# A third place in the down ring, and an up half between the down units, in a two-layer MoE decoder trunk

## The reference, cut to what matters

```python
x = layer_norm(DN_ALPHA * x + mix, ln1_g[layer], ln1_b[layer])
ff = moe_ffn(...)                       # below
x = layer_norm(DN_ALPHA * x + ff, ln2_g[layer], ln2_b[layer])

def body(y, blk):                       # in moe_ffn, for each block of tokens of one expert
    tok, wt, e = blk
    xb = x[tok]
    hb = jax.nn.silu(xb @ w_gate[e]) * (xb @ w_up[e])
    return y.at[tok].add((hb @ w_down[e]) * wt[:, None]), None
```

## Time and profile before

| | us |
|---|---|
| median of 3 runs (1247.1 to 1247.83) | 1247.29 |
| the profiled execution, its own time | 1247.77 |
| its span in the profile | 1245.9 |
| PE busy in the span | 1186.4 (95%) |
| DMA moved | 445.64 MB, mean 358 GB/s |
| the share of the w_up_ring loads in the chain that ended last | 12% |

### The profile page before, as it was taken

How to read it: one execution, slowest core, us unless ns; L and a number is a source line. 1 busy time by engine, 2 the same in 40 slices (tenths; PEclk the granted TensorE clock), 3 DMA queues, 4 the chain that set the end, 5 groups by cost and what they waited for, 6 DMA issues and landing times.

```text
span 1245.9 us, 18133 instructions
## 1 busy us (share of the span) xinstructions
PE 1186.4 (95%) x7212; PEld 544.5 (44%) x7212; DVE 396.7 (32%) x892; ACT 298.3 (24%) x652; POOL 40.5 (3%) x110
## 2 busy tenths in 40 slices
PE   8998999999999999999879999999999999999985
PEld 5776754434334343433236565343443434343421
DVE  3757374222212121212233656421221212122213
ACT  3345332211212111211121353121221211121112
POOL 1005000000000000100000000000000000010000
PEclk9999999999999999999989999999999999999998
DMA  9407159999999999999993656899999999999993
GB/s 369 172 1 302 47 220 426 403 392 427 429 429 429 429 429 428 428 428 428 426 388 128 270 203 260 352 400 396 428 429 428 429 428 429 428 428 429 429 428 156
DMA packets 44336, 445.64 MB, mean 358 GB/s; under 512 B 8064, under 2 KB 9216, under 8 KB 18176
## 3 DMA queue, kind: packets, MB, share of 16 engines
q1 hardware_dynamic: 43984, 444.71, 85.6%
q10 hardware_dynamic: 304, 0.26, 0.1%
HBM read 443.91 MB, written 1.05 MB: 357 GB/s over the span
## 4 chain that ended last, share of the span: by engine, by line
PE 80%; DMA 12%; DVE 4%; ACT 1%; issue 1%; DVEq 0%; SPq 0%
PE psum L427 31%; PE psum L508 15%; DMA w_up_ring<-in_moe_up 12%; PE psum L515 4%; PE psum L2480 4%; PE psum L441 4%; PE psum L2329 4%; PE psum L1350 3%; PE psum L659 2%; PE psum L490 1%; PE psum L1661 1%; PE psum L1833 1%; PE psum L693 1%; PE psum L2486 1%; PE psum L1397 1%
## 5 line engine op out<-in xcount | busy, mean ns | idle before, releaser
L427 PE MATMUL psum<-w_up_ring,moe_x_selected 128*64 128x512 f32 x2048 | 458.7, 596 | 17.0 <-DMA w_up_ring<-in_moe_up 11.5
L427 PEld LDWEIGHTS psum<-w_up_ring,moe_x_selected 128*64 128x64 f32 x2048 | 141.4, 137 | 298.3 <-issue 287.4
L508 PE MATMUL psum<-w_down_ring,moe_hT 128*32 128x512 f32 x1920 | 219.7, 595 | 4.3 <-DMA w_down_ring<-in_moe_down 3.4
L1181 DVE TENSOR_TENSOR moe_out_low<-psum,moe_out_high 128x512 fp32r<-128x512 f32 x128 | 88.3, 691 | 365.4 <-ACT moe_out_high L931 365.4
L931 ACT CAST moe_out_high<-psum 128x512 fp32r<-128x512 f32 x128 | 74.8, 586 | 275.3 <-PE psum L508 217.0
L1173 DVE SCALAR_TENSOR_TENSOR moe_h<-moe_silu,moe_slot_gate,psum 128x256 f32<-128x256 f32 x64 | 30.7, 480 | 290.3 <-ACT moe_silu L915 290.0
L508 PEld LDWEIGHTS psum<-w_down_ring,moe_hT 128*32 128x32 f32 x1920 | 55.7, 109 | 135.1 <-issue 125.2
L915 ACT ACTIVATE moe_silu<-psum 128x256 f32<-128x256 f32 x64 | 24.6, 384 | 226.1 <-PE psum L427 226.1
L919 ACT COPY moe_hT<-psum 128x256 f32<-128x256 f32 x64 | 23.8, 373 | 181.6 <-PE psum L490 181.6
L515 PE MATMUL psum<-moe_out_high,moe_matchT 128*128 128x512 f32 x128 | 57.6, 450 | 2.9 <-DVE moe_out_low L1181 1.9
L2329 PE MATMUL psum<-w_up_ring,mixed_transposed 128*128 128x512 f32 x128 | 56.6, 594 | 0.7 <-ACT mixed_transposed L2104 0.7
(11 more groups left out here) (538 smaller groups left out, 997.8 us busy)
## 6 DMA issues: line engine op xcount, KB each, us to landing
w_up_ring<-in_moe_up SPq DMA_DIRECT2D x128, 2048.0 KB, 18.1
w_down_ring<-in_moe_down SPq DMA_DIRECT2D x60, 2048.0 KB, 19.1
w_up_ring<-in_ev_columns SPq DMA_DIRECT2D x4, 2048.0 KB, 16.1
w_up_ring<-in_od_w_in SPq DMA_DIRECT2D x4, 2048.0 KB, 18.1
w_up_ring<-in_ev_out SPq DMA_DIRECT2D x2, 2048.0 KB, 8.3
moe_first_down<-in_moe_down SPq DMA_DIRECT2D x2, 2048.0 KB, 9.9
w_up_ring<-in_od_w_out SPq DMA_DIRECT2D x2, 2048.0 KB, 7.7
moe_shared_weights<-in_shared_up SPq DMA_DIRECT2D x1, 2048.0 KB, 7.6
```

What stands on the lines that cost most here:

```text
L427: last = nc.tensor.matmul(k.psum[e * SLOTS:(e + 1) * SLOTS, bank, :], xsel[:, kk, own:own + SLOTS], up_view(par, e, kk), start=kk == 0, st ...
L508: last = nc.tensor.matmul(k.psum[e * CAPACITY:(e + 1) * CAPACITY, unit_bank[n], :], hT[:, e // 2, own:own + CAPACITY], places[e][:, j, :], ...
L1181: nc.vector.tensor_tensor(low[:, own], k.psum[:, unit_bank[n], :], high[:, own], ALU.subtract).then_inc(s.low, 1)
```

## The change

The norm's and the tokens' tiles become one tile (`norm_and_tokens`), whose 32 KB in a partition are two half places before and one whole place now. From the second quad on, that place is the first place of every odd double (`third_down`), filled up to the seventh quad (doubles 3 to 13) and with a semaphore of its own (`x.dn_norm`). So the first down load of a double has two places, taken in turn, and is issued one double earlier. The norm's gain and bias are loaded once it is free for good, in the seventh quad, behind 30a. On PE, `down` is split into `first_two`, `third` and `last_two`, and an up half stands between units 1 and 2: 2b in the first double of a quad, the next quad's 0b in the second; ACT's silu and DVE's product of that pair move between their second and third unit. `next_up` goes behind the two combines after the gather, except in the first quad, where a part of the shared expert's product moves behind it. The last double is as before.

```diff
+    k.norm_tokens = sb("norm_and_tokens", [P, 2, NT, D])
+    k.ln, k.x = k.norm_tokens[:, 0], k.norm_tokens[:, 1]
...
+    third_ring_down = [[third_down[:, e] for e in range(4)], ring_down[1]]
...
-        refill_up(4, 4, 0)
+        for half in range(2):
+            refill_up(4, 4, half)
         refill_down(2, 1, 4)
-        refill_up(4, 4, 1)
-        refill_up(5, 5, 0)
-        refill_up(5, 5, 1)
+        for half in range(2):
+            refill_up(5, 5, half)
         refill_up(6, 6, 0)
         refill_down(2, 0, 6)
-        sp.wait_ge(s.down, 8)
-        for i, src in enumerate((d.ln2_g, d.ln2_b)):
-            sp.dma_start(k.ln[0:QUARTER, i, :], ...)
+        refill_up(6, 6, 1)
+        refill_down(3, 0, 8, third_down, x.dn_norm)
...
-        def refills(q, final=False):
-            refill_up(4 * q + 2, 2, 1)
+        def refills(q):
             for half in range(2):
                 refill_up(4 * q + 3, 3, half)
-            if not final:
-                refill_up(4 * q + 4, 0, 0)
-            for half in range(2):
-                refill_down(2 * q + 1, half, 8 * q + 2 + 2 * half)
...
+            refill_up(4 * q + 4, 0, 0)
+            refill_down(2 * q + 2, 0, 8 * q + 2)
             refill_up(4 * q + 4, 0, 1)
+            refill_down(2 * q + 1, 1, 8 * q + 4)
             for half in range(2):
                 refill_up(4 * q + 5, 1, half)
             refill_up(4 * q + 6, 2, 0)
-            for half in range(2):
-                refill_down(2 * q + 2, half, 8 * q + 6 + 2 * half)
-        refills(QUADS - 1, final=True)
+        with sp.Fori(1, QUADS - 2) as q:
+            refills(q)
+            refill_down(2 * q + 3, 0, 8 * q + 6, third_down, x.dn_norm)
+            refill_up(4 * q + 6, 2, 1)
+            refill_down(2 * q + 2, 1, 8 * q + 8)
+        q = QUADS - 2
+        refills(q)
+        sp.wait_ge(s.down, 8 * q + 6)
+        for i, src in enumerate((d.ln2_g, d.ln2_b)):
+            sp.dma_start(k.ln[0:QUARTER, i, :], ...)
+        refill_up(4 * q + 6, 2, 1)
+        refill_down(2 * q + 2, 1, 8 * q + 8)
...
+            first_two(q, 0, ring_down, landed)
+            up(q, 2, 1)
+            last_two(q, 0, ring_down, landed)
...
-                next_up(q)
             for n in (2, 3):
                 combine(q, 0, n)
...
+                next_up(q, 0)
                 pe.wait_ge(s.gates_read, q + 2)
...
+                first_two(q, 1, third_ring_down, landed)
+                next_up(q, 1)
+                last_two(q, 1, third_ring_down, landed)
```

More of the change, by code:

```diff
@@ L767, in first_quad @@
             pe.wait_ge(s.matchT, 1)
-            down(0, 0, [[first_down[:, e] for e in range(4)], ring_down[1]], [[(x.dn_first, 16)], [(x.dn1, 16)]], begin=True)
+            places, landed = [[first_down[:, e] for e in range(4)], ring_down[1]], [[(x.dn_first, 16)], [(x.dn1, 16)]]
+            first_two(0, 0, places, landed)
             up(0, 2, 1)
+            last_two(0, 0, places, landed, begin=True)
             pe.wait_ge(s.low, 3)
@@ L776, in first_quad @@
             turn(0, 3)
-            next_up(0)
-            pe.wait_ge(s.shared_h, 1)
-            combine(0, 0, 2, begin=True)
-            combine(0, 0, 3, begin=True)
-            pe.wait_ge(s.gates_read, 2)
-            down(0, 1, [ring_down[0], [place[:, e] for place in (norm_down, token_down) for e in range(2)]],
-                 [[(x.dn0, 16)], [(x.dn_norm, 16), (x.dn_tokens, 16)]])
+            next_up(0, 0)
+            shared_up(0, range(6, KD)).then_inc(s.shared_up, 1)
+            pe.wait_ge(s.gates_read, 2)
+            places, landed = [ring_down[0], third_ring_down[0]], [[(x.dn0, 16)], [(x.dn_norm, 16), (x.dn_tokens, 16)]]
+            first_two(0, 1, places, landed)
+            pe.wait_ge(s.shared_h, 1)
+            for n in (2, 3):
+                combine(0, 0, n, begin=True)
+            next_up(0, 1)
+            last_two(0, 1, places, landed)
         def quad(q, final=False):
-            landed = lambda double: [[(dn[half], 16 * (2 * q + double))] for half in range(2)]
-            up(q, 0, 1)
+            landed = [[(dn[0], 16 * (q + 1))], [(dn[1], 32 * q)]]
             pe.wait_ge(s.low, 8 * q - 1)
@@ L821, in quad @@
                 turn(q, 3)
+                landed = [[(dn[0], 16 * (q + 2))], [(dn[1], 16 * (2 * q + 1))]]
+                first_two(q, 1, ring_down, landed)
+                for n in range(2):
+                    combine(q, 1, n)
+                third(ring_down, landed)
+                pe_unit(ring_down[1], 3).then_inc(s.down, 1)
             else:
+                next_up(q, 0)
                 pe.wait_ge(s.gates_read, q + 2)
-            down(q, 1, ring_down, landed(1), final=final)
+                landed = [[(x.dn_norm, 16 * (q + 1))], [(dn[1], 16 * (2 * q + 1))]]
+                first_two(q, 1, third_ring_down, landed)
+                next_up(q, 1)
+                last_two(q, 1, third_ring_down, landed)
             if looped(q):
@@ L1190, in last_pair @@
                 read_slot_gates()
[L1191 removed]
+            if not looped(q) and q == 0:
+                shared_h(0)
+            take_low(q, 1, None if final else (q + 1, 0))
         def next_match(q):
```

118 lines of the change are left out of this document (61 added, 57 removed).

## The result

The changed kernel takes 1251.15 us (median of 11 executions, 1244.88 to 1252.98), the kernel before 1247.10 in the same comparison: a ratio of 1.0029, 95% interval 1.0017 to 1.0041. It is **slower by 0.3%**; the forecast was 0.2% faster. The profiled executions are 1251.26 and 1247.77 us, 3.5 apart.

The account below looks back on a forecast made before the run. The prediction took the queue's delivery of 31b as the bound. Queue gains of 2.4 and 1.4 us, less 0.6 in each layer for PE, gave 2.6, so 1244.7 us against 1247.29; range 1241.0 to 1247.8.

Parts of the forecast that it names:

- What bounds the kernel: Expert stages: a layer's time is set by when the queue delivers 31b; PE waits 7.7 us for loads in layer 0.
- The order in the first quad: First quad: 4b, 6a and 6b issued earlier, the queue's loss falls to 1.3 us in each layer, bounds 0 and 2.5.
- no window near 400 or less: Sign in the new profile that the forecast is right: no such GB/s window between 220 and 270 us.
- the sum of TensorE's waits: Sign in the new profile: PE's waits for loads sum to 4 or 5 us where they were 7.7.
- The gain at the queue: Less time lost in the first quad: 3.7 - 1.3 = 2.4 us in layer 0, 2.7 - 1.3 = 1.4 in layer 1.
- The step that failed: Gain and bias loads, 1.0 us, move from quad 0 to the seventh quad and cost the queue the same.
- What is late next: Stage's end, 30a to 31b: PE takes 21.1 us, the queue 20.6, so PE is about 0.6 us late in each layer.
- TensorE's switches: Breaks between units and up halves cost 0.14 us each, net +0.1 us a quad, covered by the 7.7 us of waits.
- The rival in which TensorE becomes the bound by its breaks: Rival, all quads: a break costs over 0.4 us, so the order loses; 1261 us at 0.6 us a break; chance 0.08.
- the rule on draining: Skill's rule that a change of tiling mode drains TensorE; no price given, speaks against mixing units and up halves.
- The third place: Rival: loads one double ahead don't help, all gain comes from 4b, 6a and 6b; forecast's time, no chance of its own.
- The slowest engine lost no time by waiting: Rival, first quad: its loss comes again anywhere, queue gains 0.5 us a layer at most; 1246.3 to 1247.7 us, chance 0.25.

Follow-up runs that it names:

- third_norm_last: The changed kernel with the loads of gain and bias between the last two down loads, behind 31b in the queue: 1250.88 us, ratio 1.0038.
- order_only2: The changed kernel's order in the quads without the third place, gain and bias loaded in the first quad as before: 1246.69 us, ratio 1.0004.
- order_norm_last: order_only2 with the loads of gain and bias between the last two down loads: 1257.82 us, ratio 1.0086.
- filler3: The changed kernel with three fp32 products on data nobody reads, ahead of 30a in the last quad: 1247.46 us, ratio 1.0007.
- after_again2: The changed kernel measured once more, with no edit: 1250.55 us, ratio 1.0036.
- packets8: norm and bias loads between the last two down loads, POOL clearing before copying, plus 32 unread 8 KB packets to partitions 0 to 31: 1250.60 us, ratio 1.0039.
- packets4: As packets8, but the same 0.26 MB in 64 packets of 4 KB, all from different addresses: 1252.58 us, ratio 1.0046.

## Why the prediction was wrong

*What bounds the kernel* was right for the kernel before, and is only half right for the changed one: in both layers the chain now hangs on 30a's landing, and behind that on TensorE itself.

*The order in the first quad* was right to a few tenths. SyncE's timeline of the changed kernel (compare):
```profile
219.45 0.33 SPq L268 DMA_DIRECT2D w_up_ring<-in_moe_up  x1
224.30 0.33 SPq L279 DMA_DIRECT2D w_down_ring<-in_moe_down  x1
227.87 12.83 SPq L268 DMA_DIRECT2D w_up_ring<-in_moe_up  x3
245.88 0.33 SPq L279 DMA_DIRECT2D w_down_ring<-in_moe_down  x1
250.58 0.33 SPq L268 DMA_DIRECT2D w_up_ring<-in_moe_up  x1
255.43 0.33 SPq L279 DMA_DIRECT2D norm_and_tokens<-in_moe_down  x1
259.16 0.35 SPq L268 DMA_DIRECT2D w_up_ring<-in_moe_up  x1
```
4b 219.8 was forecast and 219.45 came; the down load 246.0 and 245.88; 6b 250.7 and 250.58; the third place 255.5 and 255.43; 7a 259.1 and 259.16. But "no window near 400 or less" did not hold: 391 and 395. Of the lost time that the working kept, 1.3 us in each layer, 2.3 came in layer 0 (from 4a's landing to 7a's, less what the loads need) and 1.3 in layer 1. Nor did the sum of TensorE's waits hold, 4 or 5 us: 5.6 and 6.7.

*The gain at the queue.* Forecast was 3.7 - 1.3 = 2.4 in layer 0 and 1.4 in layer 1, with 1.0 us for gain and bias on both sides. A queue without these loads should then deliver 31b 3.4 and 2.4 us sooner; third_norm_last has exactly that queue and shows 3.5 and 3.0. In the changed kernel itself it can be read at 29b, ahead of gain and bias. What the queue had lost since 2a (the landing, less 4.895 us for each 2 MB load):

| us lost, layer 0 / 1 | at 29b | at 31b |
|---|---|---|
| before | 5.8 / 6.7 | 5.8 / 6.7 |
| order_only2 | 5.7 / 6.0 | 5.7 / 6.0 |
| changed kernel | 2.3 / 4.2 | 4.9 / 7.7 |
| third_norm_last | 2.3 / 3.7 | 2.3 / 3.7 |

So the changed kernel's queue is 3.5 and 2.6 us ahead of the one before at 29b. The term was right, within 0.6 us, but in layer 0 partly by luck: from 4a to 7a the gain is 2.5 and not 3.4, and the rest is a step of 1.0 us that the kernel before takes at 9a, with a full queue, and the changed kernel does not take. Such single steps of 1 us and more come at other loads in other traces.

***The step that failed*** is "the loads of gain and bias (1.0 us) move from quad 0 to the seventh quad; they cost the queue the same". They cost 2.6 and 3.5 us where they are now (between 29b and 31b of the changed kernel's own trace; against third_norm_last the difference in layer 1 is 4.0, but 0.5 of it was there at 29b), and next to nothing in the first quad (order_norm_last against order_only2, 0.8 us saved in one layer and 0.9 lost in the other; this was tried with the new order, not in the kernel before itself). Two errors stand in it. The size: 0.26 MB to partitions 0 to 31 costs 3 us, not 1.0. And the place: a load in a dry stretch costs nothing that shows, the same load in a full queue does. So of the 3.5 and 2.6 us that the fuller queue is ahead, these loads take 2.6 and 3.5, which leaves 0.9 and -1.0: the account's first two rows.

*What is late next.* The forecast was 0.6 us in each layer; it came to 2.1 and 2.2. The working was right but for the clock (the queue took 20.9 and 20.7 us from 30a to 31b, forecast 20.6): TensorE's 21.1 us from 30a to 31b became 23.0, of which 1.7 is 30a's product at the low clock. With the clock kept, filler3 shows 0.4 and 0.6. That a late landing at 30a makes TensorE wait and that its clock then falls was not in the working; the waits of before, at most 1.3 us each, left the clock alone there.

*TensorE's switches.* Right: an up half behind a unit takes 3.58 us, and order_only2 has all four new breaks a quad at no cost in time. The rival in which TensorE becomes the bound by its breaks falls, and with it what the rule on draining would have done to the time; a slower kernel came by another way.

*The third place* is not idle: 2.6 and 3.1 us (third_norm_last against order_norm_last), so that rival falls too.

*The slowest engine lost no time by waiting.* This rival's time, 1246.3 to 1247.7, is the nearest to what came, and its reason is partly true: in the dip of before the mean engine stood still for 1.8 us and was busy but slow for 2.1. In the changed kernel's dip it no longer stands still (a share of 1.00) and 1.7 us are still lost, with gain and bias gone from there. So that part does come again. But the queue gained 3 us all the same, which the rival denied, and it saw neither what gain and bias would cost in the new place nor the clock.

The sum, mended: layer 0 -3.5 + 2.6 + 0.4 + 1.7 = +1.2, layer 1 -2.6 + 3.5 + 0.5 + 1.7 = +3.1, together +4.3; measured between the traces 0.9 and 3.1, 4.0 in the stages, and 4.0 between the medians. The range ended at 1247.8, since the price of these loads had been given one value, 1.0, with no bound above it, though the rows of before could not tell it.

What stays open: why the delay differs between layers and executions (2.6 to 3.6 us); why single waits of about 3 us are followed by the low clock in one trace and not in another; where the loss with busy engines in the first quad comes from; and why the two loads' delay is more than the time of their own packets (64 x 0.26 / 16 = 1.0 us) by so much. The slow 16 KB packets beside them account for part, but I did not follow the single engines to the end.

## What to carry to other kernels

Before a load is moved within a queue, ask whether it lies in a dry stretch, where it may cost nothing, and what it costs in a full one: measure that by moving it out of the way, since bytes over rate said 0.6 us and the chip 3. When several changes come together, take each part's gain by a landing in the trace rather than by the total: here a gain of 3 us a stage was real and hidden under one small load and a clock. And a short load's destination counts: the same bytes spread over the partitions cost a quarter.

## What the runs showed of the hardware

- 0.26 MB written to partitions 0 to 31 in a full queue delay the loads behind by 2.6 to 3.6 us; to every fourth partition or to all of them, by 0.6 to 0.8 us. The size of the packets (4 or 8 KB to partitions 0 to 31, 8 or 2 KB spread) and the address read make no difference that shows.
- TensorE's granted clock fell to 1.2 GHz behind single waits of 2.6 and 3.8 us (changed kernel), and the next up half took 5.35 and 5.29 us instead of 3.65 (6.52 once, in after_again2). It is not the wait's length alone: in layer 0 of packets8 and packets4 waits of 3.0 and 3.1 us left the clock at 1.00 and the next product took 3.65 us, and in layer 1 of both it fell.
- Three products without use in such a wait kept the clock in the profiled execution and made the kernel about 3 us faster (ratios of 1.0029 and 1.0036 without, 1.0007 with them).
- POOL's copies of gain and bias, 3 x 1.89 us, cost nothing until something else waits for POOL behind them: then SyncE stood 15.2 us.
